# Two heads per tile on row halves, and bias with row maximum in one VectorE instruction, in the softmax attentions of a two-block transformer kernel

## The reference

```
s = jnp.einsum('bhqcd,bhkcd->cbhqk', q_blk, k).astype(jnp.float32)
...
p = jax.nn.softmax(jnp.where(allowed, s + bias, -jnp.inf), axis=-1)
...
return jnp.einsum('bhqk,bhkd->bhqd', a.astype(v.dtype), v)
```

```
s = jnp.einsum('bhqd,bhkd->bhqk', q_blk, kb).astype(jnp.float32) + bias
...
p = jax.nn.softmax(jnp.where(valid, s, -jnp.inf), axis=-1)
return jnp.einsum('bhqk,bhkd->bhqd', p.astype(vb.dtype), vb)
```

## Time and profile before

| | |
|---|---|
| time, median of 3 runs | 2241.89 us (2237.45 to 2245.74) |
| span of the profiled execution | 2243.3 us, its mean granted TensorE clock 0.948 |
| TensorE, VectorE, ScalarE busy in the span | 91%, 75%, 56% |
| diff heads | 75.2 to 160.0 us |
| band heads | 210.6 to 295.3 us |
| mixture of experts | the middle, untouched |
| nsa heads | 1816.5 to 1963.4 us |

### The profile page before, as it was taken

One profiled execution on the slowest core, in us unless ns is written; L12 is line 12 of the kernel. 1 busy time (PEld: TensorE's weight loads), 2 busy tenths in 40 slices (PEclk: granted clock), 3 DMA queues, 4 the chain that ended last, 5 costly groups with the idle time before them and its releaser, 6 DMA issues. The chain is left out here.

```text
span 2243.3 us, 29889 instructions
## 1 busy us (share of the span) xinstructions
PE 2033.7 (91%) x10236; PEld 1640.2 (73%) x10236; DVE 1684.8 (75%) x1986; ACT 1254.1 (56%) x1401; POOL 297.1 (13%) x172
## 2 busy tenths in 40 slices
PE   4988989974999999999999999999994779979998
PEld 3767768762788888888888888888883666666876
DVE  5463661266899999999999999999994446535686
ACT  3342432313677777777777777777772334352552
POOL 0202024201021211111121111212110000000000
PEclk9999999996999999999999999999997889699999
DMA  5222123426899999999999999999993611011222
GB/s 197 57 76 57 47 71 98 144 102 231 317 367 395 379 386 383 374 395 369 394 374 391 379 377 389 372 396 376 384 370 88 167 20 38 1 47 37 67 68 76
DMA packets 201621, 519.03 MB, mean 231 GB/s; under 512 B 21975, under 2 KB 81503, under 8 KB 201197
## 3 DMA queue, kind: packets, MB, share of 16 engines
q1 hardware_dynamic: 191212, 482.68, 57.9%
q0 software_dynamic: 9504, 34.61, 6.1%
q10 hardware_dynamic: 832, 0.80, 0.1%
HBM read 494.41 MB, written 29.41 MB: 234 GB/s over the span
## 5 line engine op out<-in xcount | busy, mean ns | idle before, releaser
L1681 ACT CAST moe_upper<-piece 128x2048 fp32r<-128x2048 f32 x384 | 734.1, 1914 | 282.5 <-PE bank L1613 268.4
L1761 DVE TENSOR_TENSOR piece_lower<-piece,moe_upper 128x2048 fp32r<-128x2048 f32 x384 | 869.9, 2285 | 27.3 <-ACT moe_upper L1681 27.2
L1611 PE MATMUL bank<-moe_upper,x_hi 128*128 128x512 f32 x1536 | 620.2, 404 | 2.5 <-DVE x_hi L1755 2.5
L1613 PE MATMUL bank<-moe_upper,x_hi 128*128 128x512 f32 x1536 | 605.8, 394 | 0.0
L1612 PE MATMUL bank<-piece_lower,x_hi 128*128 128x512 f32 x1536 | 601.3, 392 | 0.0
L1611 PEld LDWEIGHTS bank<-moe_upper,x_hi 128*128 128x128 f32 x1536 | 289.9, 189 | 67.8 <-DVE piece_lower L1761 2.9
L1612 PEld LDWEIGHTS bank<-piece_lower,x_hi 128*128 128x128 f32 x1536 | 290.1, 189 | 63.0
L1613 PEld LDWEIGHTS bank<-moe_upper,x_hi 128*128 128x128 f32 x1536 | 289.5, 189 | 62.5
L1565 POOL DMA_INDIRECT mixed<-moe_y,moe_dst x32 | 104.5, 3266 | 27.5 <-issue 27.5
L135 PE MATMUL bank<-x_hi,ahead_lower 128*128 128x512 f32 x256 | 102.7, 401 | 0.0
L1563 POOL COPY moe_dst<-row 128x1 uint32 (+1 forms) x32 | 6.7, 209 | 620.5 <-ACT moe_y L1670 620.5
(11 more groups left out here) (568 smaller groups left out, 3419.4 us busy)
## 6 DMA issues: line engine op xcount, KB each, us to landing
piece<-in_w_exp_in_dram SPq DMA_DIRECT2D x256, 1024.0 KB, 7.6
piece<-in_w_exp_out_dram SPq DMA_DIRECT2D x128, 1024.0 KB, 9.2
ahead<-in_w_in_dram SPq DMA_DIRECT2D x19, 512.0 KB, 4.2
ahead<-in_w_in_dram SPq DMA_DIRECT2D x3, 2048.0 KB, 7.9
ahead<-in_w_in_dram SPq DMA_DIRECT2D x4, 1536.0 KB, 6.6
merge_raw<-in_w_in_dram SPq DMA_DIRECT2D x8, 512.0 KB, 5.6
ahead<-in_w_out_dram SPq DMA_DIRECT2D x2, 2048.0 KB, 7.9
out_w<-in_w_out_dram SPq DMA_DIRECT2D x2, 2048.0 KB, 8.6
```

What stands on the lines that cost most here:

```text
L1611: nc.tensor.matmul(to, hi[:, f, :], upper[u][:, t, cols], start=f == 0 and not biased, stop=False)
L1613: done = nc.tensor.matmul(to, lo[:, f, :], upper[u][:, t, cols], start=False, stop=f == NK - 1)
L1681: nc.scalar.copy(upper[h % SPLIT][:, :, :], ring[s][:, :, :]).then_inc(hi_ready, 1)
L1761: nc.vector.tensor_tensor(lower[s][:, :, :], ring[s][:, :, :], upper[h % SPLIT][:, :, :].bitcast(F32), ALU.subtract).then_inc(lo_ready, 1)
```

## The change

A tile now holds both heads of a unit (`Pairs`; four items in a unit of diff and band, nine in nsa). The queries stay unpadded, and the two heads' scores are matmuls on 64 partitions each, into two banks. Bias and maximum are one `tensor_tensor_reduce` per head, which leaves the scores negated; exp takes them with scale -1. Diff's two maps are mixed on VectorE before the transposes, so these and the value products happen once. Band and nsa multiply with the values as the 64-column stationary side, two heads on column halves of one bank, so that the output comes out transposed: "bandt" and "nsat" are gone, and each stage's copy writes the next layout itself. In nsa, the compressed branch is one item per unit for all four row tiles (`small`), with its bias copied at the end of the stage before (`cmp_bias`). The lags are 1, 2 and 3 items; the projected bank is a single one (`PROJECTED`), read out before the next. The casts and splits of "nsat" move to ScalarE and GpSimd in the nsa stage (`beside`), and SyncE issues those 2 MB first.

```diff
-LOOK, NORM_LAG, COPY_LAG, PV_LAG = 2, 2, 3, 4
+NORM_LAG, TURN_LAG, VALUE_LAG, RING = 1, 2, 3, 4
+TURNED, WEIGHED, PROJECTED, FIRST_PROJECTED = (4, 5), 6, 7, (7, 2)
...
+def pair_scores(k, t, keys):
+
+    first = 1024 * (t % 2)
+    return k.psum[:, first:first + 1024].rearrange("p (m x) -> p m x", m=2)[:, :, 0:keys]
...
-            nc.tensor.matmul(k.bank[t % 2][:, 0:it["keys"]], it["q"](u), it["kt"](u), start=True, stop=True)\
-                .then_inc(b["scored"], 1)
+            to = pair_scores(k, t, it["keys"])
+            for first, width, cols in it["parts"]:
+                for m in range(2):
+                    last = nc.tensor.matmul(to[:, m, first:first + width], it["q"](u, m)[:, cols], it["kt"](u, m),
+                                            start=True, stop=True)
+            last.then_inc(b["scored"], 1)
             projection(u + 1, items.place(t))
...
+                for j, rows, cols in it["weighs"]:
+                    for m in range(2):
+                        last = nc.tensor.matmul(to[HD * m:HD * m + HD, it["cols"]], it["v"](u, m, j),
+                                                pt[0:rows, m, cols], start=it["first"] and j == 0,
+                                                stop=it["last"] and j == it["weighs"][-1][0])
...
-            nc.vector.tensor_tensor(s, k.bank[t % 2][:, 0:it["keys"]], it["bias"](u), ALU.add)
-            dve.drain()
-            nc.vector.tensor_reduce(b["nm"][:, t % 4:t % 4 + 1], s, AX.X, ALU.max, negate=True)\
-                .then_inc(b["biased"], 1)
+                for m in range(2):
+                    last = nc.vector.tensor_tensor_reduce(
+                        out=e[:, m, :], in0=pair_scores(k, t, keys)[:, m, :], in1=it["bias"](u)[:, m, :], scale=-1.0,
+                        scalar=BEYOND, op0=ALU.add, op1=ALU.min, accum_out=nm[:, m:m + 1])
+                last.then_inc(b["biased"], 1)
...
+                if items.mixed:
+                    nc.vector.tensor_tensor(l[:, 1:2], l[:, 1:2], it["scale"](u, 1), ALU.mult)
+                    nc.vector.tensor_scalar(e[:, 0, :], e[:, 0, :], l[:, 0:1], None, ALU.mult)
+                    dve.drain()
+                    nc.vector.scalar_tensor_tensor(out=e[:, 1, :], in0=e[:, 1, :], scalar=l[:, 1:2], in1=e[:, 0, :],
+                                                   op0=ALU.mult, op1=ALU.add).then_inc(b["normed"], 1)
...
+                for m in range(2):
+                    last = nc.scalar.activation(e[:, m, :], e[:, m, :], ACT.Exp, bias=b["nm"][:, t % RING, m:m + 1],
+                                                scale=-1.0, accum_out=b["l"][:, t % RING, m:m + 1])
...
         @block.sync
         def _(sp):
+            if beside is not None:
+                following(sp)
             for u in range(done, units):
...
-            if following is not None:
+            if following is not None and beside is None:
                 sp.wait_ge(projected, projected0 + units * projections)
                 following(sp)
...
+                    if u > 0 and n == 1:
+                        pe.wait_ge(evacuated, evacuated0 + 2 * u + 1)
```

More of the change, by code:

```diff
@@ L20 @@
 NEG = -1e30
+BEYOND = 3e38
 LN_EPS = 1e-5
@@ L456, in attention_pe @@
+        if 0 <= n < N:
+            it = items.item(n)
+            e = b["e"][:, n % RING, :, :]
             pe.wait_ge(b["normed"], at + n + 1)
-            if a >= 2:
-                pe.wait_ge(b["copied"], at + n + 1 - 2 * maps)
-            for j, rows in items.blocks(n):
-                last = nc.tensor.transpose(k.bank[3 + a % 2][0:rows, j * P:(j + 1) * P],
-                                           b["scores"][:, n % 4, j * P:j * P + rows], k.ident)
-            last.then_inc(b["transposed"], maps)
@@ L463, in attention_pe @@
-        n = t - PV_LAG
-        if 0 <= n < N and items.summed(n):
-            it, u = items.tile(n), items.unit(n)
-            pe.wait_ge(b["copied"], at + n + 1)
-            if it["first"] and items.opens(n):
-                pe.wait_ge(b["out_copied"], b["out_done"] + u * NT + it["i"] + 1)
-            col, width = it["out"]
-            blocks = items.blocks(n)
-            for j, rows in blocks:
-                last = nc.tensor.matmul(k.bank[5 + it["i"] % 2][:, col:col + width],
-                                        b["pt"][0:rows, n // maps % 3, j * P:(j + 1) * P], it["v"](u, j),
-                                        start=it["first"] and j == 0, stop=it["last"] and j == len(blocks) - 1)
-            last.then_inc(b["weighed"], maps)
@@ new lines, in attention_pe @@
+        n = t - VALUE_LAG
+        if 0 <= n < N:
+            it, u = items.item(n), items.unit(n)
+            pt = b["pt"][:, n % 2, :, :]
+            pe.wait_ge(b["copied"], 2 * (at + n + 1))
+            if u > 0 and items.place(n) == 0:
+                pe.wait_ge(b["out_copied"], b["out_done"] + 2 * u)
+            to = k.bank[WEIGHED]
+            if items.mixed:
+                blocks = key_blocks(it["keys"])
+                for j, rows in blocks:
+                    last = nc.tensor.matmul(to[:, it["cols"]], pt[:, 0, j * P:(j + 1) * P], it["v"](u, 0, j),
+                                            start=j == 0, stop=j == len(blocks) - 1)
+            else:
+                for j, rows, cols in it["weighs"]:
[3 more added lines that the diff above has]
+                                                stop=it["last"] and j == it["weighs"][-1][0])
+            last.then_inc(b["weighed"], 1)
@@ L529, in attention_act @@
+def attention_act(nc, act, k, items, b, weights, next_queries, copy_out):
+    N, at = items.n, b["at"]
+    for t in range(N + VALUE_LAG + 1):
         if t < N:
-            if items.place(t) == items.per_unit - 1:
-                next_unit(items.unit(t) + 1)
-            s = b["scores"][:, t % 4, 0:items.tile(t)["keys"]]
+            it = items.item(t)
+            e = b["e"][:, t % RING, :, 0:it["keys"]]
             act.wait_ge(b["biased"], at + t + 1)
-            nc.scalar.activation(s, s, ACT.Exp, bias=b["nm"][:, t % 4:t % 4 + 1],
-                                 accum_out=b["l"][:, t % 4:t % 4 + 1]).then_inc(b["exped"], 1)
@@ L749, in heads_stage @@
-    k.units.counted(w0_in=loads * ((units + 1) // 2 - done), w1_in=loads * (units // 2),
-                    w_split=(units - done) * projections, projected=(units - done) * projections, evacuated=2 * units, zeroed=1, v_hi=NT if early else 0, v_ps=len(v_rows), v_sb=len(v_rows))
-def first_attention_stage(nc, name, k, w, first_q, first_k, bias, shared_v, scale, out, maps=1, following=None,
-                          projected_values=False):
+            next_keys(0)
+            attention_dve(nc, dve, k, items, b, next_keys, copy_out, keys is not None and upper_out is not None)
```

401 lines of the change are left out of this document (233 added, 168 removed).

## The result

The changed kernel takes 2150.57 us (median of 4 runs, 2149.37 to 2153.57) against 2242.82 of before, measured beside it: a ratio of 0.9591, 95% interval 0.9577 to 0.9606. The forecast was 2158 with a range of 2125 to 2200.

The account below looks back on a forecast made before the run. TensorE's passes bound diff and band except their last units; VectorE's work and hand-over per tile bound NSA. Savings 15.5 + 11.2 + 5.7 + 45.4 + 5.6 = 83.4 off 2242 gave 2158 us, range 2125 to 2200.

Parts of the forecast that it names:

- three units save 9, the last 6.5: Diff heads: three TensorE-bound units take 18 for 20.9 us, the last 15.5 for 22.0; together 15.5 saved.
- the edge between row modes: TensorE, attention items: each change between half and full tiling costs about 0.1 us, three or four per item.
- tail of 6: Last band unit: exp through output copy of the last tile take 6 us after VectorE's 8.6, about as before.
- the load order: NSA start: the 2 MB issued ahead of the second unit's query weights delays the first split product by 6.6 us.
- 4 of cold clock: NSA heads: 4 us added for TensorE's cold clock at the start, beside units of 28, 28, 26 and a tail.
- an engine that is idle there: NSA heads: GpSimd takes over the removed transposing stage's splits while idle; that stage's removal saves 5.6 us.
- 1.3 us of bias copies: End of the stage before NSA: four added bias copies cost 1.3 us.
- Rival C: Fused instruction at the scan's rate or below: 0.46 more per 512, 5.3 per NSA unit, 2179; chance 0.13.
- B: Band and NSA values: column halves run one after the other, 2178; chance 0.18 together with a half clock in NSA's last unit.
- D: NSA: load not late (6.6) and hand-overs free (6), 2145; with cheap row and column halves down to 2125; chance 0.06.
- F: Wait between two-head tiles eats the whole gain: 25 us more per NSA unit, 1 per other, 2241; chance 0.03.
- E: TensorE's clock granted at 0.5 through the three head stages, doubling 185 us of bound units: 2343; chance 0.02.

Follow-up runs that it names:

- the split experiment: Changed kernel with the four lower parts of the stick-breaking weights made by VectorE instead of GpSimd: 2149.20 us, ratio 0.9589 to the kernel before.

## Why the prediction was right

The mechanism was right and no rival came true; the time came out 7 us below the forecast because the saving in NSA was undersized, and that band came out near its forecast is in part luck.

**Diff.** The step "three units save 9, the last 6.5" gave 15.5; 15.4 was measured, the units at 16.4, 18.5 and 18.5 for the 18 forecast and the last at 16.0 for 15.5. The halved scores, the halved transposes and values, and a keys' copy that TensorE waits 0.34 to 1.0 for are as priced. So is the edge between row modes: the full-height pass behind the scores at 86.41 takes 0.34 until the next begins, for 0.23 in the steady row, 0.1 as forecast; the rule of the Trainium skill on a change of mode (TensorEngine Tiling (Array Packing), Key Properties) agrees with it in kind.

**Band.** 11.2 forecast, 9.3 measured, and the two parts missed by more, in opposite directions. The three units with a projection took 55.7 (16.1, 19.8 and 19.8) and saved 7.0, where the forecast had 1.5 each, 4.5. The last unit took 19.6 (248.81 to 268.41) and saved 2.3, where the forecast had 14.8 and 6.7. The mis-sized term is its tail of 6, taken from a kernel whose last tile is one head. Behind the last maximum are now 9.2 us:

```profile
259.24:268.41 9.17, 5.79 (x50) 4.64 (x50) 2.57 (x8) 4.67 (x11) 0.00 (x0) 0.81 0.01 2
```

Before, from the end of the last maximum (288.82 plus 0.69) to the last copy (295.29) were 5.8. The last item now has exp, scaling, transposes, copies and values of two heads behind that maximum. The part ahead of it took 10.4 for the 8.6 of VectorE's work.

**The fused instruction.** Priced at 0.69 and 0.1, measured at 0.69 and 0.08. The rule of the Trainium skill that I weighed against it (Vector Engine (DVE) Microarchitecture Reference, Points that are easy to get wrong, on two SBUF sources that are not bf16) did not show with one source in PSUM; no run here has both sources of the fused instruction in SBUF. The mix of diff's maps, a scalar_tensor_tensor without a second output, does have both there, in fp32, and takes 0.75 at 512 keys, a tenth more than the add:

```profile
139.25 0.75 DVE L548 SCALAR_TENSOR_TENSOR diff_scores<-diff_scores,diff_l 128x512 f32<-128x512 f32 x1
```

The prediction did not price the instruction by itself. Alone in the kernel of before it is 40 us. In NSA VectorE is busy 24.7 less for the 32 saved, and the other 7.6 come with a clock of 1.00 in the last unit. Undone in the changed kernel it is 23.

**NSA.** The stage saved 52.4 for the 45.4 forecast, and this is the term that was mis-sized. The first split product came 15.0 after the last compressed copy (forecast 15.2, before 8.6). The forecast put the load order at 6.6 of it; the difference to before is 6.4, and the experiment with the weights first gives 5.9. From there to the end were 86.5, not 93. The second unit took 28.6 for 28, and the last with its tail 33.3 for 26 and 7, as forecast; all of the miss is in the first, 24.6 for 28 and 4 of cold clock. Its clock was 0.92 in the mean, which costs about 2 (an estimate: 0.08 of 24.6), not 4. The rest, some 5, looks counted twice in the sum (read off the counts, not tested): with transposes and values two and three items late, the first unit's window holds 129 matmuls and the second's 205. A unit's late work lies in the next window, and only the last unit's in the tail of 7, so the first window had to be the shorter one. The step that said GpSimd's splits move "into an engine that is idle there" overlooked that they stretch VectorE's scalings by 6.7 us; it was harmless, as the split experiment shows.

**A term that I had the wrong way.** The prediction names 1.3 us of bias copies lost at the end of the stage before (its 1824.7 is 1818.10 plus 6.6 and leaves them out); they took 1.0, and 5.2 were won there all the same. ScalarE now copies the first queries before it waits for the next weights (`next_queries(0, ...)` ahead of `upper_part(1, n)`), and the first score starts 1.9 after the last compressed copy instead of 7.0. It shortens nothing by itself: TensorE then stands 11.25 us for the split weights, whose landing sets the first split product.

**Slips in the working.** VectorE had 31 us a unit before (92.45 over three), not 33. Band's last unit adds up to 8.5 and 6, 14.5, not 14.8. Rival C's 0.46 for 512 is 4.6 to 4.8 an NSA unit, not 5.3. None moves the forecast by more than 0.3.

**The rivals.** B fell (0.058 a pass on alternating halves), C fell (0.69), D's condition did not hold (the small transfers took 9.1 to land behind the 2 MB and 3.6 ahead of them). F fell with the time itself, and ScalarE set no unit: it is busy 19.0 of 28.6 us in the second. E, the clock, is the one that came nearest to being real: 0.98 in band and 0.96 in NSA cost little, but with both heads on one row half the same kernel has 0.62 in its first and 0.70 in its last NSA unit, and the stage loses 35 us, some 22 of them (the estimate above) with the clock.

## What to carry to other kernels

Where TensorE waits on a chain of other engines, a shorter chain can pay twice, in its own time and in the clock: here 24.7 and 7.6 us. The clock is not to be guessed from the load, though: more work on TensorE went with 1.00 in one experiment and with 0.50 in another. Forecast such a stretch at both levels, and let a run decide. A busy share of 92% beside a wait on another engine does not say who is the bound; putting one pass back in does. When a large load is moved ahead of small ones on a queue, follow the small ones to the engine that waits for them: here the order alone was 6 us. And in a pipeline with lags, count the work that runs late once, either in the next unit or in the tail.

## What the runs showed of the hardware that was not expected

- The granted clock of a stretch with TensorE busy throughout was 0.50 (both heads' scores on one row half, 1900 to 1920), and three added products per tile turned 0.50 into 1.00 from 1910 to 1950 in the kernel of before. What exactly in the load decides between the two was not separated.
- A VectorE scaling from SBUF to SBUF beside a GpSimd split took until the split ended (2.77 us for a pair that takes 0.73 without it), while the fused instruction, with one source in PSUM, was at most 0.69 in all 112 of its uses, some of them beside such a split (two of 0.69 at 105.72 and 106.34, beside the split from 105.12 to 107.51).
- Value passes on one column half start 0.11 apart, as those of full width do; ordered head by head they still overlapped in part, 0.089 a pass, against 0.058 alternating.
